# One core of a Trainium2 chip: the down product of a mixture-of-experts slice runs two gate and up steps behind instead of one

## The reference

```python
def swiglu(h, w1, w3, w2):
    return (jax.nn.silu(h @ w1) * (h @ w3)) @ w2

def moe_swiglu(h, w_router, w1, w3, w2):
    ...
    top_logit, top_e = lax.top_k(logits, TOP_K)
    gates = jax.nn.softmax(top_logit, axis=-1)
    ...
    def expert_block(args):
        xi, e = args
        return swiglu(xi, w1[e], w3[e], w2[e])

    yb = lax.map(expert_block, (xb, block_e)).reshape(n_rows, D)
    y = jnp.zeros_like(x).at[sorted_tok].add(sorted_gate[:, None].astype(x.dtype) * yb[dest])
```

## Time and profile before

| | |
|---|---|
| time, median of 3 runs | 2563.68 us (2563.45 to 2566.68) |
| span of the profiled execution | 2562.7 us |
| around the span, against the median | 1.0 us |
| PE busy | 2467.0 us, 96% of the span |
| mean granted TensorE clock | 0.981 |
| the eight units on PE | about 1175 to 2531 us of the span |

### The profile page before, as it was taken

How to read it: one execution, slowest core, us unless ns; L and a number is a source line. 1 busy time by engine, 2 the same in 40 slices (tenths; PEclk the granted TensorE clock), 3 DMA queues, 4 the chain that set the end, 5 groups by cost and what they waited for, 6 DMA issues and landing times.

```text
span 2562.7 us, 38680 instructions
## 1 busy us (share of the span) xinstructions
PE 2467.0 (96%) x16200; PEld 2157.5 (84%) x16201; DVE 661.1 (26%) x1405; ACT 507.9 (20%) x1034; POOL 116.0 (5%) x100
## 2 busy tenths in 40 slices
PE   8999998999999999999989999999989989999998
PEld 5668647888876578648989998999989989999996
DVE  2256544333742366422000000010000000100104
ACT  2145522222430255411001001011010010100102
POOL 2020100000000030101000000000000000000001
PEclk9999998999999999999999999999999999999999
DMA  8200444333220210535785656778767767787883
GB/s 259 82 34 15 138 141 127 99 99 123 91 84 27 82 48 1 174 112 215 296 306 191 227 197 232 294 264 300 294 249 262 275 252 291 296 312 296 321 302 117
DMA packets 202899, 482.32 MB, mean 188 GB/s; under 512 B 4834, under 2 KB 31601, under 8 KB 202337
## 3 DMA queue, kind: packets, MB, share of 16 engines
q1 hardware_dynamic: 192240, 430.41, 45.7%
q0 software_dynamic: 8304, 40.82, 5.1%
q10 hardware_dynamic: 2176, 8.39, 0.8%
HBM read 460.98 MB, written 35.39 MB: 194 GB/s over the span
## 4 chain that ended last, share of the span: by engine, by line
PE 81%; issue 2%; DVE 1%; ACT 0%; DVEq 0%; ACTq 0%
PE ps L922 34%; PE ps L937 17%; PE ps L821 10%; PE ps L657 6%; PE ps L832 4%; PE ps L665 3%; PE ps L773 2%; PE ps L650 2%; PE ps L906 1%; PE ps L878 1%; PE ps L890 1%; PE ps L753 0%; PE ps L754 0%; PE ps L1005 0%; PE ps L748 0%
## 5 line engine op out<-in xcount | busy, mean ns | idle before, releaser
L922 PE MATMUL ps<-hT,attention_arena 128*128 128x128 f32 (+4 forms) x4096 | 525.5, 286 | 35.0 <-issue 35.0
L922 PEld LDWEIGHTS ps<-hT,attention_arena 128*128 128x128 f32 x4096 | 510.5, 194 | 36.8 <-issue 36.8
L1616 DVE TENSOR_TENSOR attention_arena<-ps,attention_arena 128x256 f32<-128x256 f32 x224 | 95.2, 425 | 1215.4 <-ACT attention_arena L1209 1215.4
L922 PE MATMUL ps<-hT,weight_ring 128*128 128x128 f32 (+4 forms) x3072 | 388.6, 283 | 0.0
L922 PEld LDWEIGHTS ps<-hT,weight_ring 128*128 128x128 f32 x3072 | 376.8, 191 | 0.0
L1209 ACT ACTIVATE attention_arena<-ps 128x256 f32<-128x256 f32 x224 | 85.9, 383 | 1128.7 <-PE ps L922 1128.6
L937 PE MATMUL ps<-attention_arena 128*128 128x128 f32 (+4 forms) x2048 | 266.1, 283 | 0.0
L657 PE MATMUL ps<-weight_ring,hT 128*128 128x384 f32 (+3 forms) x768 | 257.8, 496 | 3.5 <-DMA weight_ring<-in_w_in_dram 1.8
L937 PEld LDWEIGHTS ps<-attention_arena 128*128 128x128 f32 x2048 | 254.1, 191 | 0.0
L657 PEld LDWEIGHTS ps<-weight_ring,hT 128*128 128x128 f32 x768 | 146.4, 192 | 106.2 <-issue 61.4
L821 PE MATMUL ps<-x_high,w_parts 128*128 128x512 f32 x704 | 224.0, 399 | 5.5 <-ACT x_high L1104 5.5
(11 more groups left out here) (203 smaller groups left out, 1837.9 us busy)
## 6 DMA issues: line engine op xcount, KB each, us to landing
attention_arena<-in_e_w_dram SPq DMA_DIRECT2D x96, 2048.0 KB, 12.2
weight_ring<-in_e_w_dram SPq DMA_DIRECT2D x72, 2048.0 KB, 12.2
weight_ring<-in_w_dram SPq DMA_DIRECT2D x22, 1024.0 KB, 6.8
weight_ring<-in_w_dram SPq DMA_DIRECT2D x4, 2816.0 KB, 9.7
weight_ring<-in_w_o_dram SPq DMA_DIRECT2D x4, 2048.0 KB, 8.3
attention_arena<-rows_by_slot POOLq DMA_DIRECT2D x8, 1024.0 KB, 11.3
results_by_slot<-attention_arena ACTq DMA_DIRECT2D x8, 1024.0 KB, 9.8
weight_ring<-in_w_in_dram SPq DMA_DIRECT2D x2, 3072.0 KB, 10.5
```

The costliest lines, as they stand in the source:

```text
L922: last = nc.tensor.matmul(ps[:, f % 2, m * UNIT:m * UNIT + n], w[:, k, i * P:(i + 1) * P], XT[:, k, 0:n], start=(k == 0), stop=(k == ND - 1))
L1616: tt(eh[:, f % EHS, :], ps[:, f % 2, UNIT:2 * UNIT], esil[:, f % 2, :], ALU.mult).then_inc(gu_free, 1)
```

## The change

The down step that follows the gate and up step f is f - 2 and no longer f - 1. In a unit's first two pieces no down step runs, and at its end the down steps 26 and 27 stand behind the last turn.

```diff
@@ -81,6 +81,7 @@
 EHS = 4
+BEHIND = 2
 GIVEN_GU, GIVEN_FREE, GIVEN_Y, GIVEN_TURN = FE, 4, 4, 2
@@ -951,11 +952,12 @@
                     if f == FE - 1:
                         next_rows_turned(u, 0)
                         next_rows_turned(u, 1)
-                    if f:
-                        down_step(u, f - 1, n)
+                    if f >= BEHIND:
+                        down_step(u, f - BEHIND, n)
                 next_rows_turned(u, 2)
                 next_rows_turned(u, 3)
-                down_step(u, FE - 1, n)
+                for f in range(FE - BEHIND, FE):
+                    down_step(u, f, n)
                 return back
```

## The result

| | before | after |
|---|---|---|
| median | 2564.52 us (2563.45 to 2566.68, 4 runs) | 2595.91 us (2595.07 to 2598.34, 4 runs) |
| span of the profiled execution | 2562.7 us | 2594.3 us |
| mean granted TensorE clock | 0.981 | 0.978 |

The changed kernel is slower by 31.4 us, a ratio of 1.0125 (95% interval 1.0112 to 1.0138). The forecast was 2611 us, 15 us too high, with the time inside its range.

What follows compares the result with a forecast made beforehand. PE was taken as the bound, losing 35.0 us of issue ahead of units; 37 us at seven ends, 3 at the last and 7 for the clock, together 47 us on 2563.7, gave 2611 us, range 2561 to 2640.

Steps and rivals of the forecast that it cites:

- Waits in a unit: Inside a unit, the dropped down-step wait and the third gate and up step's wait on VectorE: nothing, 1.3 us to spare.
- weights: Loads into weight slots: down slots come free 3.6 us later, next load due 32 us later; priced at nothing.
- a longer run ahead: Unit ends: a second down step behind the last turn hides more issue; forecast no gain, faster rival 2555 us, chance 0.05.
- The place of the branch: Unit end: branch to the head falls 25 instructions into the twelfth block, so a block is entered between hint and branch.
- Its price: Cost of the lost head at the branch: 5.3 us at each of seven ends between units, 37 us in sum.
- the head, which was the last thing loaded, no longer is: Unit end: entering the twelfth block loads the one behind it after the hinted head, so the head is lost.
- 14 instruction loads, the head twice among them: Sign that the forecast is right: instruction loads in a unit, where 13 would do.
- if the head is asked for on entering the last block: Bound for the branch's cost: asked for 25 instructions, 1.4 us, earlier, so 4.6 us of 6.0 remain.
- the last end: End of the last unit, where no weights are loading: half of 6, 3 us.
- the clock: Lower granted clock in first steps behind longer pauses: 2.4 us at each of three starts that become long, 7 us.
- the head stays: Rival at the unit-end branch: the hinted block is kept, branch takes 0.34 us; 2564 to 2568 us, chance 0.28.
- The second rival: Unit end: the hint also pushes out the twelfth block, 9.2 us an end, seven times; 2644 us, chance 0.20.

## Why the prediction was right, and what in it was not

**Waits in a unit, weights, a longer run ahead: nothing.** Right. PE shows no wait but issue, and the sequencer passes the branch's placing at 1329.3, 2.2 us ahead of the end of the last down step (1331.46), the same lead as before (1329.4 to 1331.60). The order by itself is worth nothing either way: ratio 0.9995 with the branch deep in its block.

**The place of the branch.** Right, and what decided the sign. The count is borne out by the hint at place 50, which brought the short branch back in all five units where place 50 could be met, and by the placing of the hint: it no longer jumps a block in units of 128 rows (202 ns at most, 434 before), as place 74 ahead of 80 says.

**Its price.** This is the mis-sized term. The step "the head, which was the last thing loaded, no longer is" was wrong as a picture: the head had not been loaded at all. From it came "14 instruction loads, the head twice among them" (there are 3 fewer in all, not more) and a price between 4.6 and 6.0 us. The text had the right case among its bounds, "if the head is asked for on entering the last block", and took the middle instead. Even that bound was too high, since it carried over the 6.0 us of the long branches, which are two loads in a row, while here it is one load, late. Measured: 4.32 - 0.34 = 4.0 us a branch, and 26.1 / 7 = 3.7 us an end on PE, so 26 instead of 37. With 0.8 instead of 3 at the last end (one load without weights: 1.43 us), and 4.1 instead of 7 for the clock, the three sizes are 16 us too high together, which is the forecast's excess of 15 within a microsecond.

**What was luck.** The picture of a head that is loaded and then lost calls for a loss wherever a block is entered between hint and branch; with the branch 145 instructions into its block there was none (2563.23 us). That the wrong picture gave the right sign was luck: the branch happened to lie only 25 instructions into its block. That the time lies in the range says little, since the range also held a kernel that is not slower. Of the signs that were named, a branch of 3 to 7 us came at seven of the eight ends, and no short start is left (4.08 us is the shortest pause); issue grew to 61.1 us and not over 70, and the head was not loaded twice.

**The rivals.** That the head stays as in the kernel before is refuted by L991. Whether a block loaded by hint outlives an entry, the point on which that rival turned, was not what decided: nothing had been loaded that could be kept. The second rival (the last block lost as well) is refuted by the same counts: one load is missed and no more, and the last two down steps run through without a gap (3.60 us for both).

Its rule, two blocks held and the next one loaded ahead, is that of the Trainium skill, "Runtime: NRT & Kernel Launch", section "Instruction fetch mechanics". By that rule the forecast's text had the hint's block displace the twelfth; here the hint had loaded nothing by then, and the head took the place of the thirteenth, which is not loaded at these ends. How many blocks are held, no run here shows.

## What to carry to other kernels

A hint for a branch works only once the block that holds the branch is current (a hint with more than one entry into a block ahead of its branch was not run): count the instructions between that block's start (or the hint, if later) and the branch, not between hint and branch, and recount whenever an edit moves 32 of them. Loads of code wait while data fill the transfer engines, so a transfer that is not urgent is best issued behind a jump to far code, not ahead of it: here that gave 0.4%. Where a pause is made of loads, look up how many are in it before its length is used as a price for one.

## What was not expected of the hardware

- A hint ahead of its branch's block loaded nothing for 9.7 us, though the queues were empty for the last 5.5 of them; the load started about 0.5 us behind the entry into the block, and the block behind was then not loaded (150 loads against 158 without a hint).
- From entry to the end of the branch it took some 3.3 us with no weights flowing (1.4, 0.3 for the placing, 1.6), and 6.0 with them (1.4 + 0.3 + 4.3), at a transfer share of 105% from 1328 to 1330 us.
- A long branch behind an end of a unit takes 6.2 to 6.8 us among weights and rows in the kernel before, where two loads start while it waits; it takes 3.3 to 3.7 us with both held back (four starts), where the first of the two starts 0.7 to 1.9 us ahead of it.
